# A streaming encoder step on one core: VectorE's lane marks, the sample's last v rows and the second norms

## The chip, the core and the metric

One NeuronCore of a Trainium2 chip runs the whole program in one launch. The metric is the device time of that launch in microseconds (us); below, "time" is always that. The engines are TensorE (PE; PEld is its weight load), VectorE (DVE), ScalarE (ACT), GpSimd (POOL) and SyncE (SP).

## What is computed

The reference runs one layer over a prompt of 512 frames and a sample of 64 frames with a cache of 1024 rows, width 1024, all in float32:

```python
h = x @ w_in                                   # q, k, v of 8 forgetting heads and 4 differential heads, and a gate
x = LayerNorm(alpha*x + concat(A, B) @ w_out)  # A, B: the two attentions
x = LayerNorm(alpha*x + PEER(x))               # ln2_g, ln2_b
# PEER, for each block of 128 frames
q = (xs @ w_pq).reshape(128, 8, 2, 128);  sc = einsum('thpd,hpnd->thpn', q, sub_keys)
s, i = top_k(sc, 16);  top, sel = top_k(pair sums of s, 16);  eidx = the chosen pairs' expert numbers
g = softmax(top)
hid = einsum('td,thkd->thk', xs, u_tab[eidx]);  a = g * gelu(hid)
out = einsum('thk,thkd->td', a, v_tab[eidx])   # 128 experts a frame, each a row of 1024 floats in two tables
```

Returned are y, the new k and v rows and the log forget gates.

## The kernel before

**Blocks and slots.** There are four prompt blocks (p = 0 to 3) of 128 frames and the sample (p = 4, `SMP`, 64 frames). Each prompt block needs 128 experts a frame: 128 *slots*. In the sample two experts of one frame share a pass (its 64 frames stand twice in the 128 partitions), so it has 64. That makes 576 slots. For each slot k GpSimd issues two indirect gathers of 128 rows x 4 KB = 512 KB: the u row (`peer_u`) and the v row (`peer_v`), both at line 2063. VectorE multiplies the u rows with x and sums (L1988, `hid`), ScalarE makes the coefficient (L1498, L1506) and, for slots that TensorE takes, a diagonal matrix of it (L1527). TensorE adds diag x v row into PSUM (L1173, two 128x512 matmuls, which the trace shows as four records); for the other slots VectorE adds coef x v row into `y_acc` in SBUF (L2000). Which slot goes where is `on_tensor(k)`: all 64 of the sample's go to TensorE.

**The order.** Every engine's program is one woven list. The slot lane "j" makes one step a mark: at mark j GpSimd gathers u row j and v row j-8, VectorE takes u row j-3, and row j-11 is added to the sum. All other work is cut into lanes with a fixed number of steps spread over a range of marks (`STAGES`, `SEARCH`, `spans`, `weave`): "x" the projections, "a" attention, "o"/"m" the output projection and first norm, "w" the queries and key scores, "t" VectorE's top-k search and decoding, "f" and "n" the second norm. So the lanes' marks alone set what stands between two u rows on VectorE and between two v rows on TensorE. Block p changes to p+1 at slots 128, 256, 384 and 512. "x" of block 2 makes the projections of block 2, block 3 and the sample together (`shared_tensor`): 2 steps for the gate, 16 for v, 32 for q and k, 4 empty.

**Buffers.** u rows have 6 buffers (7 from slot 288, 9 from 376), v rows 6 (9 from 282, 12 from 372). A gather waits for its buffer's last user. Weights stream on SP's queue through a ring of 5 tiles of 512 KB; the first four v tiles lie in `held`. x of the block is read by the u step from SBUF (`x1`), or, in the ranges of `MID` and from slot 408 on, from a copy in PSUM (`x_mid`, `mixer` in the trace).

**The second norm.** `f_vector` (L2015 to L2021) adds the PSUM sum to `y_acc` and takes mean and variance. PE's `n_tensor` puts gain and bias into PSUM by matmuls (L726). `n_vector` in its first step does (y - mean) x rstd over 1024 columns (L2027, L2028) and in its second waits for the gain (`ln2_row`) and does y x gain (L2031) and y + bias (L2033, L2034). SP stores y (L720). For the sample all of this stands behind the last row.

**The forgetting sums.** `sample_forget` at marks 266 to 275 takes the running sum of 1024 cached gates on VectorE (L1602).

## Time and profile before

| | |
|---|---|
| median of 3 runs | 1904.21 us (1901.42 to 1924.45) |
| profiled execution | 1909.52 us, of it 1907.7 us between first and last instruction |
| busy | PE 81%, DVE 68%, POOL 65%, ACT 32% |
| moved | 712.21 MB, mean 373 GB/s |
| mean granted clock of TensorE | 0.911 |

In the rows, busy time is in us, a bracket behind an instruction is the idle time before it and what ended it, and a stretch A:B is given in us from the first instruction. "issue" is a wait that nothing in the profile explains, "remote" one whose releaser isn't known. A gather's row is GpSimd's own time for it; its data land later.

### The profile page before, as it was taken

The numbers are of one execution on the slowest core, as the hardware profiler recorded it, in microseconds if no ns is written. First come the engines' busy times: TensorE is split into PE (matmuls) and PEld (weight loads), VectorE is DVE, ScalarE is ACT, GpSimd is POOL, SyncE is SP. The second block draws the span as 40 slices with busy tenths as digits, with TensorE's granted clock in tenths as the row PEclk, the third lists the DMA queues.
The fourth block names the chain that finished last, engine by engine and source line by source line (L and its number), as shares of the span: only waits on it lengthen the run. The fifth ranks groups of instructions, "written<-read, shape, count | busy, mean of one in ns | idle before, by whom it ended". The sixth has DMA issues, their size and how long they took to land. (4 is left out here: it accounts for less than half of the span.)

```text
span 1907.7 us, 18411 instructions
## 1 busy us (share of the span) xinstructions
PE 1542.1 (81%) x5192; PEld 819.3 (43%) x5192; DVE 1294.9 (68%) x2822; ACT 611.0 (32%) x1725; POOL 1247.6 (65%) x1199
## 2 busy tenths in 40 slices
PE   8998878959997788887979879896487776657767
PEld 7586444713454344653534534662132222222223
DVE  2378866379878775778898776778686566554443
ACT  1422363223222453234754631232232122112221
POOL 3026666677687766666677676777776666776663
PEclk9999889969998899888989989998798988888898
DMA  9899999999999999999999999999999999999995
GB/s 304 308 338 335 388 344 374 403 396 365 391 409 408 412 367 345 409 405 410 360 348 405 398 409 409 385 409 397 360 376 368 380 349 374 393 368 354 373 385 222
DMA packets 204093, 712.21 MB, mean 373 GB/s; under 512 B 24696, under 2 KB 31640, under 8 KB 203864
## 3 DMA queue, kind: packets, MB, share of 16 engines
q0 software_dynamic: 166720, 605.75, 82.5%
q1 hardware_dynamic: 37272, 105.28, 14.8%
q8 instruction: 43, 0.70, 0.1%
q14 instruction: 58, 0.48, 0.1%
HBM read 703.79 MB, written 7.74 MB: 373 GB/s over the span
## 5 line engine op out<-in xcount | busy, mean ns | idle before, releaser
L2063 POOL DMA_INDIRECT ubuf<-in_peer_u,idx x495 | 533.3, 1077 | 235.7 <-issue 146.3
L2063 POOL DMA_INDIRECT vbuf<-in_peer_v,idx x444 | 481.6, 1085 | 262.3 <-issue 115.5
L1173 PE MATMUL acc<-vbuf,diag 128*128 128x512 f32 x968 | 525.3, 677 | 140.6 <-DMA vbuf<-in_peer_v,idx 79.5
L1988 DVE CUSTOM_DVE_ANT_0 ubuf<-ubuf,x 128x1024 f32<-128x1024 f32 x304 | 369.8, 1225 | 124.3 <-DMA ubuf<-in_peer_u,idx 90.6
L1173 PEld LDWEIGHTS acc<-vbuf,diag 128*128 128x128 f32 x968 | 191.0, 212 | 387.0 <-issue 368.3
L1988 DVE CUSTOM_DVE_ANT_0 ubuf<-ubuf,mixer 128x1024 f32<-128x1024 f32 x191 | 230.1, 1217 | 109.4 <-issue 52.2
L1498 ACT ACTIVATE act_h<-hid 128x4 f32<-128x4 f32 x144 | 29.6, 205 | 537.7 <-issue 319.9
L2000 DVE SCALAR_TENSOR_TENSOR y_acc<-vbuf,coef,y_acc 128x1024 f32<-128x1024 f32 x138 | 177.3, 1285 | 34.7 <-DMA vbuf<-in_peer_v,idx 24.4
L1150 PEld LDWEIGHTS mixer<-stage,wring 128*128 128x128 f32 x1024 | 135.8, 197 | 20.5 <-issue 18.1
L1150 PE MATMUL mixer<-stage,wring 128*128 128x128 f32 (+1 forms) x1024 | 137.7, 293 | 5.7 <-issue 3.7
L1506 ACT ACTIVATE coef<-act_h,g 128x1 f32<-128x1 f32 x576 | 122.6, 283 | 17.3 <-ACT act_h L1498 1.1
L1527 ACT ACTIVATE diag<-ident,coef 128x128 f32<-128x128 f32 x320 | 115.5, 395 | 4.7 <-ACT coef L1506 0.9
L2063 POOL DMA_INDIRECT held<-in_peer_v,idx x81 | 84.1, 1038 | 36.5 <-issue 24.9
L1173 PE MATMUL acc<-held,diag 128*128 128x512 f32 x132 | 70.4, 668 | 29.7 <-DVE y_acc L2015 13.7
L1173 PE MATMUL acc<-vbuf,xT 128*128 128x512 f32 x120 | 65.1, 672 | 25.0 <-DMA vbuf<-in_peer_v,idx 13.1
L1988 DVE CUSTOM_DVE_ANT_0 wring<-wring,mixer 128x1024 f32<-128x1024 f32 x38 | 46.0, 1219 | 47.1 <-issue 16.7
L899 PE MATMUL mixer<-kv,stage 128*128 128x64 f32 (+1 forms) x320 | 49.0, 286 | 31.6 <-ACT x L1309 17.3
L778 PE MATMUL mixer<-stage,wring 128*128 128x320 f32 x256 | 71.9, 433 | 0.0
L2063 POOL DMA_INDIRECT wring<-in_peer_v,idx x51 | 48.6, 952 | 30.4 <-remote 17.0
L1498 ACT ACT_TABLE_LOAD x52 | 66.7, 1283 | 0.9
L778 PEld LDWEIGHTS mixer<-stage,wring 128*128 128x128 f32 x256 | 48.9, 191 | 26.4 <-issue 8.9
L1458 ACT COPY stage<-mixer 128x256 f32<-128x256 f32 (+1 forms) x32 | 12.8, 399 | 146.1 <-PE mixer L1150 85.7
(351 smaller groups left out, 2161.8 us busy)
## 6 DMA issues: line engine op xcount, KB each, us to landing
wring<-in_w_pq SPq DMA_DIRECT2D x64, 512.0 KB
wring<-in_w_qk SPq DMA_DIRECT2D x34, 512.0 KB
wring<-in_w_out SPq DMA_DIRECT2D x32, 512.0 KB
ubuf<-in_peer_u,idx POOLq DMA_INDIRECT x495
vbuf<-in_peer_v,idx POOLq DMA_INDIRECT x444
wring<-in_w_v SPq DMA_DIRECT2D x12, 512.0 KB
wring<-in_c_k SPq DMA_DIRECT2D x8, 512.0 KB
wring<-in_c_v SPq DMA_DIRECT2D x8, 512.0 KB
```

The lines of the kernel that those rows point to most:

```text
L778: last = pe.matmul(mixer[:, at:at + XN], w[:, c, :], xs[:, c, :], start=c == 0, stop=c == KT - 1)
L899: last = pe.matmul(head_sums(p, m, width), pT2[m % 2][:, c, :], vS[:, c, col:col + width], start=c == 0, stop=c == nk // P - 1)
L1150: last = pe.matmul(ps_o[:, t % 2, j * cols:(j + 1) * cols], w[:, c, :], x1T[:, c, :], start=c == 0, stop=c == KT - 1)
L1173: last = pe.matmul(sums[hf], diags[D_PLAN[n][0]], v_buf[b][:, hf * 512:(hf + 1) * 512], start=first, stop=last_one)
L1458: nc.scalar.copy(qh[h % 2][:, 0:2 * cols], ps_o[:, h % 2, 0:2 * cols]).then_inc(qh_out, 1)
L1498: nc.scalar.activation(act_h[:, c:c + GRP], hid[:, c:c + GRP], ACT.Gelu).then_inc(gelu_done, 1)
L1506: last = nc.scalar.activation(coef[:, c + i:c + i + 1], act_h[:, c + i:c + i + 1], ACT.Copy, scale=g[p % 2][:, at + i:at + i + 1])
L1527: nc.scalar.activation(diags[b], (ident2 if p == SMP else ident)[:, :], ACT.Copy, scale=coef[:, v % MARKS:v % MARKS + 1]).then_inc(diag_do ...
L1988: nc.vector.tensor_tensor_reduce(out=u, in0=u, in1=x, scale=1.0, scalar=0.0, op0=ALU.mult, op1=ALU.add, accum_out=hid[:, k % MARKS:k % MAR ...
L2000: nc.vector.scalar_tensor_tensor(y_acc[p % 2][:, :], v_buf[b], coef[:, v % MARKS:v % MARKS + 1], y_acc[p % 2][:, :], ALU.mult, ALU.add).th ...
L2063: pool.indirect_dma_start(buf, None, a[table], bass.IndirectOffsetOnAxis(ap=idx[p % 2][:, at:at + 1], axis=0)).then_inc(landed_, 16)
```

## The change

1. VectorE's search steps leave the marks behind a change of blocks: the third piece of block 1 runs over marks 142 to 182 (130 to 176 before), of block 2 over 270 to 308 (258 to 306), of block 3 over 399 to 440 (392 to 436), and its first two are drawn together to 350 to 366 and 366 to 384. The first norm of block 3 ("m") and the sample's stages move by 1 to 2 marks, the norm steps of block 1 are 4 marks apart instead of 1.5.
2. The 54 steps of the shared projections are spaced by weight: 18 over marks 93 to 118, 32 over 118 to 154, 4 over the rest.
3. The running sum of the cached gates is taken at marks 226 to 231 into a place of its own.
4. Of the sample's last 16 slots, the 8 odd ones go to VectorE, into block 3's `y_acc` (`y_late`). TensorE starts the sample's sum with alpha x (2 matmuls, ScalarE's pass over y falls away) and ends it with ident2 x y_late (2 matmuls).
5. The second norms are written as two passes of two halves: (y - mean) x gain, then x rstd + bias. The first now waits for `ln2_row`. The sample's reads its sum straight from PSUM, uses block 3's gain and bias, and is stored in two halves.

```diff
-SEARCH = {1: ((13, 70, 90), (21, 90, 130), (21, 130, 176)),
-          2: ((13, 211, 226), (21, 226, 258), (21, 258, 306)),
-          3: ((13, 350, 372), (21, 372, 392), (21, 392, 436))}
+SEARCH = {1: ((13, 70, 90), (21, 90, 130), (21, 142, 182)),
+          2: ((13, 211, 226), (21, 226, 258), (21, 270, 308)),
+          3: ((13, 350, 366), (21, 366, 384), (21, 399, 440))}
+SHARE = ((18, 93, 118), (32, 118, 154), (4, 154, 156.5))
+def mix_marks(lo):
+    return [lo + m for m in (2.0, 3.2, 4.4, 7.4, 8.4, 9.0)]
...
     if p == SMP:
-        return True
+        return at < DEC - 16 or at % 2 == 0
     if at < 3:
...
-          3: ((226, 231), (232, 268), (268, 275), (), (350, 436)),
-          SMP: ((266, 275), (276, 314), (314, 343), (343, 367), (436, 478))}
+          3: ((226, 231), (232, 268), (268, 277.5), (), (350, 440)),
+          SMP: ((266, 275), (278, 315), (315, 344), (344, 367), (442, 482))}
...
         out.append(("f", p, 1, end + 1.0 + late, end + 2.0 + late))
-        rows, to = ((224.0, 231.0), (368.0, 371.0), (400.0, 410.0), (end + 4.0 + late, end + 14.0 + late), (end + 4.0, end + 7.0))[p]
+        rows, to = ((224.0, 231.0), (367.5, 375.5), (400.0, 410.0), (end + 4.0 + late, end + 14.0 + late), (end + 4.0, end + 7.0))[p]
         out.append(("n", p, 2, rows, to))
...
             at = [m for piece in SEARCH[p] for m in even(*piece)]
+        elif (name, p) == ("x", SHARED):
+            at = [m for piece in SHARE for m in even(*piece)]
+        elif name == "m":
+            at = mix_marks(lo)
         elif (name, p) == ("o", SMP):
...
+        lf_sum = held[96:96 + FOX_HEADS, 0, :]
...
+        gain_s = stage[:, 0:D]
+        y_late = y_acc[(SMP - 1) % 2]
...
         def y_store(sp, p):
             frames = DEC if p == SMP else P
+            dst = o["y"][p * P:p * P + frames, :]
+            if p == SMP:
+                for hf, made in enumerate((y_half, y_done)):
+                    sp.wait_ge(made, NB if hf else 1)
+                    c = slice(hf * 512, (hf + 1) * 512)
+                    sp.dma_start(dst[:, c], y_acc[p % 2][0:frames, c]).then_inc(out_y[p % 2], 16)
+                return
             sp.wait_ge(y_done, p + 1)
-            sp.dma_start(o["y"][p * P:p * P + frames, :], y_acc[p % 2][0:frames, :]).then_inc(out_y[p % 2], 16)
+            sp.dma_start(dst, y_acc[p % 2][0:frames, :]).then_inc(out_y[p % 2], 16)
...
                         pe.wait_ge(y_done, SMP - 1)
+                        for hf in range(2):
+                            pe.matmul(sums[hf], ident_a[:, :], x1[SMP % 3][:, hf * 512:(hf + 1) * 512], start=True, stop=False)
                     elif first:
...
                         last = pe.matmul(sums[hf], diags[D_PLAN[n][0]],
-                                         v_buf[b][:, hf * 512:(hf + 1) * 512], start=first, stop=last_one)
+                                         v_buf[b][:, hf * 512:(hf + 1) * 512], start=first and p < SMP,
+                                         stop=last_one and p < SMP)
                     last.then_inc(vP_used, 1)
+                if v == JSLOTS - 1:
+                    pe.wait_ge(vD_used, JSLOTS - PE_COUNT[JSLOTS])
+                    for hf in range(2):
+                        last = pe.matmul(acc_s[hf], ident2[:, :], y_late[:, hf * 512:(hf + 1) * 512], start=False, stop=True)
+                    last.then_inc(late_done, 1)
                 yield
         def n_tensor(pe, p):
+            if p == SMP:
+                yield
+                yield
+                return
             pe.wait_ge(sc_out, HEADS * min(p + 3, SMP))
...
                             act.wait_ge(out_y[p % 2], 16 * (p // 2))
-                        nc.scalar.mul(y_acc[p % 2][:, :], x1[p % 3][:, :], ALPHA).then_inc(acc_made, 1)
+                        if p < SMP:
+                            nc.scalar.mul(y_acc[p % 2][:, :], x1[p % 3][:, :], ALPHA).then_inc(acc_made, 1)
                     if on_tensor(v):
...
         def f_scalar(act, p):
+            if p == SMP:
+                act.wait_ge(ln2_row, SMP)
+                for hf in range(2):
+                    nc.scalar.copy(gain_s[:, hf * 512:(hf + 1) * 512], ps_o[:, hf, :]).then_inc(gain_in, 1)
             act.wait_ge(ln2_v, p + 1)
...
                 if t == 2:
-                    dve.wait_ge(lf_in, 16)
                     dve.wait_ge(s_done, MATS * SMP)
-                    link(nc.vector.tensor_tensor_scan(dd[:, 0:PAST], lf_past, lf_past, 0.0, ALU.add, ALU.bypass))
-                    link(nc.vector.tensor_copy(carry[:, :], dd[:, PAST - 1:PAST]))
+                    dve.wait_ge(lf_summed, 1)
+                    link(nc.vector.tensor_copy(carry[:, :], lf_sum[:, PAST - 1:PAST]))
                     link(nc.vector.tensor_tensor_scan(dd[:, PAST:PAST + DEC], lf_wait[:, XCOLS[SMP]], lf_wait[:, XCOLS[SMP]],
...
                  yield
         def x_vector(dve, p, chain):
...
                 else:
-                    for _ in range(x_steps(p)):
-                        yield
+                    yield
+                    dve.wait_ge(lf_in, 16)
+                    nc.vector.tensor_tensor_scan(lf_sum, lf_past, lf_past, 0.0, ALU.add, ALU.bypass).then_inc(lf_summed, 1)
+                    yield
                 return
...
                     dve.wait_ge(coef_done, v // GRP + 1)
-                    if n == p * SLOTS - PE_COUNT[p * SLOTS]:
+                    first = n == p * SLOTS - PE_COUNT[p * SLOTS]
+                    if first and p == SMP:
+                        dve.wait_ge(out_y[(SMP - 1) % 2], 32)
+                    elif first:
                         dve.wait_ge(acc_made, p + 1)
...
                     dve.wait_ge(v_in[b], 16 * (nth + 1))
-                    nc.vector.scalar_tensor_tensor(y_acc[p % 2][:, :], v_buf[b], coef[:, v % MARKS:v % MARKS + 1],
-                                                   y_acc[p % 2][:, :], ALU.mult, ALU.add).then_inc(vD_used, 1)
+                    by = coef[:, v % MARKS:v % MARKS + 1]
+                    y = y_late if p == SMP else y_acc[p % 2]
+                    if first and p == SMP:
+                        nc.vector.tensor_scalar(y[:, :], v_buf[b], by, None, ALU.mult).then_inc(vD_used, 1)
+                    else:
+                        nc.vector.scalar_tensor_tensor(y[:, :], v_buf[b], by, y[:, :], ALU.mult, ALU.add).then_inc(vD_used, 1)
                 yield
         def f_vector(dve, p, chain):
...
             end = min((p + 1) * SLOTS, JSLOTS)
-            dve.wait_ge(vP_used, PE_COUNT[end])
-            wait(dve, vD_used, end - PE_COUNT[end])
             if p == SMP:
-                dve.wait_ge(acc_made, NB)
-            if p == SMP:
-                for hf in range(2):
-                    last = nc.vector.tensor_tensor(y[:, hf * 512:(hf + 1) * 512], y[:, hf * 512:(hf + 1) * 512], acc_s[hf], ALU.add)
+                dve.wait_ge(late_done, 1)
+                sums = acc_s
             else:
-                last = nc.vector.tensor_tensor(y[:, :], y[:, :], acc[:, :], ALU.add)
-            last.then_inc(acc_read, 1)
-            dve.wait_ge(acc_read, p + 1)
+                dve.wait_ge(vP_used, PE_COUNT[end])
+                wait(dve, vD_used, end - PE_COUNT[end])
+                nc.vector.tensor_tensor(y[:, :], y[:, :], acc[:, :], ALU.add).then_inc(acc_read, 1)
+                dve.wait_ge(acc_read, p + 1)
+                sums = [y[:, hf * 512:(hf + 1) * 512] for hf in range(2)]
             for hf in range(2):
-                last = nc.vector.bn_stats(stats2[:, n, hf, :], y[:, hf * 512:(hf + 1) * 512])
+                last = nc.vector.bn_stats(stats2[:, n, hf, :], sums[hf])
             link(last)
...
         def n_vector(dve, p, chain):
             link, y, n = chain.link, y_acc[p % 2], p % 2
+            gain, bias_n = (ps_o2, acc_p) if p >= SMP - 1 else (ps_s[:, 0:D], acc_s)
+            dve.wait_ge(ln2_v, p + 1)
+            if p == SMP:
+                dve.wait_ge(out_y[p % 2], 16 * (p // 2))
+                dve.wait_ge(gain_in, 2)
+            else:
+                dve.wait_ge(ln2_row, p + 1)
+            for hf in range(2):
+                c = slice(hf * 512, (hf + 1) * 512)
+                was, by = (acc_s[hf], gain_s[:, c]) if p == SMP else (y[:, c], gain[:, c])
+                link(nc.vector.scalar_tensor_tensor(y[:, c], was, mv2[:, n, 0:1], by, ALU.subtract, ALU.mult))
             dve.wait_ge(ln2_r, p + 1)
             link(nc.vector.reciprocal(rstd2[:, n, 1:2], rstd2[:, n, 0:1]))
-            link(nc.vector.tensor_scalar(y[:, :], y[:, :], mv2[:, n, 0:1], rstd2[:, n, 1:2], ALU.subtract, ALU.mult))
-            yield
-            dve.wait_ge(ln2_row, p + 1)
-            link(nc.vector.tensor_tensor(y[:, :], y[:, :], ps_o2 if p >= SMP - 1 else ps_s[:, 0:D], ALU.mult))
-            bs = acc_p if p >= SMP - 1 else acc_s
-            link(nc.vector.tensor_tensor(y[:, 0:512], y[:, 0:512], bs[0], ALU.add))
-            nc.vector.tensor_tensor(y[:, 512:D], y[:, 512:D], bs[1], ALU.add).then_inc(y_done, 1)
+            yield
+            for hf in range(2):
+                c = slice(hf * 512, (hf + 1) * 512)
+                last = nc.vector.scalar_tensor_tensor(y[:, c], y[:, c], rstd2[:, n, 1:2], bias_n[hf], ALU.mult, ALU.add)
...
+            last.then_inc(y_done, 1)
             yield
...
```

The first place is VectorE about the end of block 1 (its PSUM sum is read at L2015, L2063 after); `y_acc1` is block 1's sum, `sc`, `top_v`, `best_i`, `cand` are the search. Before:

```order
L2000 SCALAR_TENSOR_TENSOR y_acc0<-vbuf,coef,y_acc0 128x1024 [waits v_in4,acc_made,coef_done]
L1893 MAX top_v<-sc 128x8 [waits sc_out] x2
L1885 MAX_INDEX best_i<-best_v,cand2 128x8
L1897 TENSOR_TENSOR cand<-top_v 128x256
L2015 TENSOR_TENSOR y_acc1<-y_acc1,acc 128x1024 [waits vD_used,vP_used,dve_link]
L2019 BN_STATS stats2<-y_acc1 128x6 [waits acc_read]
L2019 BN_STATS stats2<-y_acc1 128x6
L2021 BN_AGGR mv2<-stats2 128x2 [waits dve_link]
L1988 ISA ubuf,hid<-ubuf,x1_2 128x1024 [waits u_in1]
L1988 ISA hid 128x1
L2000 SCALAR_TENSOR_TENSOR y_acc0<-vbuf,coef,y_acc0 128x1024 [waits v_in5,vD_used,coef_done]
```

After:

```order
L2051 SCALAR_TENSOR_TENSOR y_acc0<-vbuf,coef,y_acc0 128x1024 [waits v_in4,acc_made,coef_done]
L2063 TENSOR_TENSOR y_acc1<-y_acc1,acc 128x1024 [waits vD_used,vP_used]
L2067 BN_STATS stats2<-y_acc1 128x6 [waits acc_read]
L2067 BN_STATS stats2<-y_acc1 128x6
L2069 BN_AGGR mv2<-stats2 128x2 [waits dve_link]
L2031 ISA ubuf,hid<-ubuf,x1_2 128x1024 [waits u_in1]
L2031 ISA hid 128x1
L2051 SCALAR_TENSOR_TENSOR y_acc0<-vbuf,coef,y_acc0 128x1024 [waits v_in5,vD_used,coef_done]
L2031 ISA ubuf,hid<-ubuf,x1_2 128x1024 [waits u_in2]
L2031 ISA hid 128x1
L2051 SCALAR_TENSOR_TENSOR y_acc0<-vbuf,coef,y_acc0 128x1024 [waits v_in0,vD_used,coef_done]
L1643 COPY carry<-held 8x1 [waits lf_summed,s_done]
```

The search rows ahead of the sum are gone, and the scan has become a copy (L1643); the slots' own rows stand as they did, and the search is taken up again three u rows later.

The second place is VectorE at mark 225, the first step of block 0's norm, with what each instruction waits for. Before:

```order
L1988 ISA ubuf,hid<-ubuf,x1_1 128x1024 [waits u_in0,pick_done]
L1988 ISA hid 128x1
L2027 RECIPROCAL rstd2<-rstd2 128x1 [waits ln2_r]
L2028 TENSOR_SCALAR y_acc0<-y_acc0,mv2,rstd2 128x1024 [waits dve_link]
L1988 ISA ubuf,hid<-ubuf,x1_1 128x1024 [waits u_in1,dve_link]
L1988 ISA hid 128x1
L2000 SCALAR_TENSOR_TENSOR y_acc1<-vbuf,coef,y_acc1 128x1024 [waits v_in5,vD_used,coef_done]
L1893 MAX top_v<-sc 128x8 [waits sc_out] x2
```

After:

```order
L2031 ISA ubuf,hid<-ubuf,x1_1 128x1024 [waits u_in0,pick_done]
L2031 ISA hid 128x1
L2084 SCALAR_TENSOR_TENSOR y_acc0<-y_acc0,mv2,mixer 128x512 [waits ln2_row,ln2_v]
L2084 SCALAR_TENSOR_TENSOR y_acc0<-y_acc0,mv2,mixer 128x512 [waits dve_link]
L2086 RECIPROCAL rstd2<-rstd2 128x1 [waits ln2_r,dve_link]
L2031 ISA ubuf,hid<-ubuf,x1_1 128x1024 [waits u_in1,dve_link]
L2031 ISA hid 128x1
L2051 SCALAR_TENSOR_TENSOR y_acc1<-vbuf,coef,y_acc1 128x1024 [waits v_in5,vD_used,coef_done]
L1936 MAX top_v<-sc 128x8 [waits sc_out] x2
```

Before, `ln2_row` was awaited four u rows later, at L2031; now it is awaited ahead of them. The scan of the cached gates (L1663) has come in behind the second step.

The third place is VectorE's end: the last u rows and the sample's norm. Before:

```order
L1988 ISA wring,hid<-wring,mixer 128x1024 [waits x_copied,u_in8]
L1988 ISA hid 128x1
L2013 TENSOR_TENSOR y_acc0<-y_acc0,mixer 128x512 [waits acc_made,vD_used,vP_used]
L2013 TENSOR_TENSOR y_acc0<-y_acc0,mixer 128x512
L2019 BN_STATS stats2<-y_acc0 128x6 [waits acc_read]
L2019 BN_STATS stats2<-y_acc0 128x6
L2021 BN_AGGR mv2<-stats2 128x2 [waits dve_link]
L2027 RECIPROCAL rstd2<-rstd2 128x1 [waits ln2_r]
L2028 TENSOR_SCALAR y_acc0<-y_acc0,mv2,rstd2 128x1024 [waits dve_link]
L2031 TENSOR_TENSOR y_acc0<-y_acc0,mixer 128x1024 [waits ln2_row,dve_link]
L2033 TENSOR_TENSOR y_acc0<-y_acc0,acc 128x512 [waits dve_link]
L2034 TENSOR_TENSOR y_acc0<-y_acc0,acc 128x512 [waits dve_link]
```

After:

```order
L2051 SCALAR_TENSOR_TENSOR y_acc1<-held,coef,y_acc1 128x1024 [waits v_in6,vD_used,coef_done]
L2051 SCALAR_TENSOR_TENSOR y_acc1<-held,coef,y_acc1 128x1024 [waits v_in8,vD_used,coef_done]
L2051 SCALAR_TENSOR_TENSOR y_acc1<-vbuf,coef,y_acc1 128x1024 [waits v_in1,vD_used,coef_done]
L2051 SCALAR_TENSOR_TENSOR y_acc1<-vbuf,coef,y_acc1 128x1024 [waits v_in3,vD_used,coef_done]
L2051 SCALAR_TENSOR_TENSOR y_acc1<-vbuf,coef,y_acc1 128x1024 [waits v_in5,vD_used,coef_done]
L2067 BN_STATS stats2<-mixer 128x6 [waits late_done]
L2067 BN_STATS stats2<-mixer 128x6
L2069 BN_AGGR mv2<-stats2 128x2 [waits dve_link]
L2084 SCALAR_TENSOR_TENSOR y_acc0<-mixer,mv2,stage 128x512 [waits gain_in,out_y0,ln2_v]
L2084 SCALAR_TENSOR_TENSOR y_acc0<-mixer,mv2,stage 128x512 [waits dve_link]
L2086 RECIPROCAL rstd2<-rstd2 128x1 [waits ln2_r,dve_link]
L2090 SCALAR_TENSOR_TENSOR y_acc0<-y_acc0,rstd2,acc 128x512 [waits dve_link]
```

Five v rows stand behind the last u row, the sum is awaited once (`late_done`), and the passes over y between the sum and the store have become four of half the width.

## Rows read from the trace of the kernel before

**Rows 1.** The page, part 2: GB/s in 40 slices of the span

```profile
GB/s 304 308 338 335 388 344 374 403 396 365 391 409 408 412 367 345 409 405 410 360 348 405 398 409 409 385 409 397 360 376 368 380 349 374 393 368 354 373 385 222
```

**Rows 2.** Stretches: length, busy PE, PEld, DVE, ACT, POOL (instructions), clock, DMA share, GB/s

```profile
440.00:480.00 40.00, 40.00 (x86) 13.54 (x87) 36.88 (x90) 13.06 (x35) 31.34 (x26) 1.00 0.95 347
...
960.00:1010.00 50.00, 37.15 (x96) 17.46 (x95) 46.56 (x107) 25.60 (x54) 38.92 (x34) 0.86 0.97 353
1310.00:1340.00 30.00, 23.52 (x48) 8.28 (x47) 23.35 (x81) 5.95 (x19) 23.29 (x23) 0.98 1.00 385
1340.00:1370.00 30.00, 12.53 (x24) 4.75 (x22) 18.83 (x46) 7.55 (x19) 20.50 (x21) 0.82 0.95 358
1370.00:1410.00 40.00, 31.94 (x64) 12.94 (x64) 39.52 (x101) 14.87 (x50) 31.44 (x28) 0.84 0.95 351
...
1840.00:1860.00 20.00, 12.48 (x26) 4.44 (x26) 9.40 (x17) 4.37 (x17) 14.05 (x15) 1.00 1.03 412
```

**Rows 3.** GpSimd's gathers by buffer, 1800 to 1860: busy us, mean ns, idle

```profile
L2063 POOL DMA_INDIRECT ubuf<-in_peer_u,idx x15 | 14.1, 937 | 4.6 <-issue 4.0 <-DVE hid L1988 0.6
```

**Rows 4.** Timeline of GpSimd at 1360: start, us, idle before

```profile
1361.70 0.94 POOL L2063 DMA_INDIRECT ubuf<-in_peer_u,idx  x1 [1.98 <-DVE hid L1988]
...
1364.78 0.94 POOL L2063 DMA_INDIRECT ubuf<-in_peer_u,idx  x1 [0.90 <-DVE hid L1988]
```

**Rows 5.** Timeline: VectorE's first norm step, TensorE's gain and bias, blocks 0 to 3; the scan

```profile
845.06 0.16 DVE L2027 RECIPROCAL rstd<-rstd 128x1 f32<-128x1 f32 x1
...
847.51 4.16 PE L726 MATMUL mixer<-d_neg,ident 32*128 32x512 f32 x8
...
1285.04 0.15 DVE L2027 RECIPROCAL rstd<-rstd 128x1 f32<-128x1 f32 x1
...
1284.06 3.81 PE L726 MATMUL mixer<-d_neg,ident 32*128 32x512 f32 x8
...
1390.02 0.15 DVE L2027 RECIPROCAL rstd<-rstd 128x1 f32<-128x1 f32 x1
...
1388.34 3.69 PE L726 MATMUL mixer<-d_neg,ident 32*128 32x512 f32 x8
...
1752.30 0.16 DVE L2027 RECIPROCAL rstd<-rstd 128x1 f32<-128x1 f32 x1
...
1756.23 1.87 PE L726 MATMUL acc<-d_neg,ident 32*128 32x512 f32 x4
...
981.10 2.28 DVE L1602 TENSOR_TENSOR_SCAN d_neg<-held 8x1024 f32<-8x1024 f32 x1
```

**Rows 6.** Timeline of the end: a late gather, TensorE's last rows, VectorE's norm, the store

```profile
1873.51 0.93 POOL L2063 DMA_INDIRECT held<-in_peer_v,idx  x1 [0.31 <-issue]
...
1881.57 5.39 PE L1173 MATMUL mixer<-held,xT 128*128 128x512 f32 x12 [2.12 <-DMA held<-in_peer_v,idx]
...
1886.80 10.46 PE L1173 MATMUL mixer<-vbuf,diag 128*128 128x512 f32 x24
...
1897.30 1.28 DVE L2013 TENSOR_TENSOR y_acc<-y_acc,mixer 128x512 f32<-128x512 f32 x2 [15.72 <-PE mixer L1173]
1898.62 1.29 DVE L2019 BATCH_NORM_STATS2 stats<-y_acc 128x6 f32<-128x512 f32 x2
...
1900.51 0.16 DVE L2027 RECIPROCAL rstd<-rstd 128x1 f32<-128x1 f32 x1 [0.36 <-ACT rstd L1533]
...
1903.53 0.69 DVE L2034 TENSOR_TENSOR y_acc<-y_acc,acc 128x512 f32<-128x512 f32 x1
1904.25 0.49 SPq L720 DMA_DIRECT2D out_y<-y_acc  x1
```

**Rows 7.** Timeline of VectorE: a v row, and a wait whose releaser isn't known

```profile
1372.24 1.28 DVE L2000 SCALAR_TENSOR_TENSOR y_acc<-wring,coef,y_acc 128x1024 f32<-128x1024 f32 x1
...
1783.63 1.22 DVE L2031 TENSOR_TENSOR y_acc<-y_acc,mixer 128x1024 f32<-128x1024 f32 x1 [18.46 <-remote]
```

**Rows 8.** Timeline of TensorE: one v row after a long wait

```profile
1374.71 3.78 PE L1173 MATMUL acc<-held,diag 128*128 128x512 f32 x4 [13.70 <-DVE y_acc L2015]
```

17 lines of the change are left out of this document (12 added, 5 removed).

## The prediction

> **What bounds the kernel now.** I read the page first, for its 40 slices. In nearly half of them the DMA engines move over 385 GB/s, and no slice goes above 412 [rows 1]. The best stretches do the same: 412 between 1840 and 1860 us [rows 2]. I take 410 as full speed. The slots read 1152 gathers of 512 KB, so one gather is 524288 B / 410 GB/s = 1.28 us of transfer and a slot 2.56. All 712.21 MB would take 1737 us; the profiled execution takes 1909.52. So the kernel is bound by its transfers, and what can be won is the 170 us in which they fall short of 410. A stretch loses its length x (1 - GB/s / 410). That is the scale for everything below: taking an instruction off VectorE, TensorE or ScalarE wins nothing by itself, only what it gives back to the gathers.
>
> Next I read the stretches with low GB/s, with each engine's busy time [rows 2]. 440 to 480 us (slots 98 to 111) loses 6.1 us, 960 to 1010 (slots 264 to 280) loses 50 x (1 - 353/410) = 7.0, 1310 to 1340 loses 1.8, 1340 to 1370 loses 3.8 and 1370 to 1410 loses 5.8 (together slots 378 to 412). The engine to watch is GpSimd. A gather costs it 0.937 us and 0.31 us of "issue" before the next [rows 3]: 4.6 us idle for 15, or 1.24 us each, just under the 1.28 of the transfer. But in the losing stretches a gather takes longer: 31.34/26 = 1.205 us, 38.92/34 = 1.145, 31.44/28 = 1.123, 23.29/23 = 1.013 [rows 2]. With 0.31 added, the first makes 1.52 us, and 26 x 1.52 = 39.4 of 40 us: GpSimd is full. What differs is VectorE: there it takes x from SBUF beside the u row, in 1840 to 1860 from PSUM, and it is busy 36.88 of 40 us instead of 9.40 of 20.
>
> The Trainium skill (page "SBUF — State Buffer", section "Who interferes with whom") says that VectorE and GpSimd share one pair of ports under an exclusive lock, which VectorE takes when it reads two operands from SBUF. The 1.205 against 0.937 us agree with it. By that rule only VectorE's instructions with two SBUF operands would matter, not its busy share. I keep to the measured means.
>
> Two other views close this part. GpSimd's own timeline shows where VectorE's u rows come late: waits of 1.98 and 0.90 us at 1360 [rows 4]. And from 1440 on every 30 to 40 us some engine stands still without a releaser; the longest row is VectorE's 18.46 us before the second norm step of block 3, though TensorE's gain was written at 1758.10 [rows 5, 7].
>
> **The change, part by part.**
>
> (A) Shared projections. Between 440 and 480 TensorE is busy 40.00 of 40 us, and GpSimd is full too [rows 2]. 18 steps over marks 93 to 118 instead of 21 marks take load off TensorE per slot, at most the 6.1 us lost there. But GpSimd stays full as long as VectorE holds it up, and the part gets 4 slots longer, each 3.03 us instead of 2.56, or with what is denser behind it about +1.5. I take 0 (from -6.1 to +1.5): with two engines full, relief of one gives nothing.
>
> (B) Change from block 1 to block 2. The search rows leave VectorE for marks 270 to 308, and the scan of 2.28 us [rows 5] goes. Nothing is less in sum; the work comes where u rows leave room. If a gather there fell from 1.145 to 1.013 us, the least loaded of these stretches, that is 34 x 0.132 = 4.5 us. The ends are 0 and -7.0, all that is lost. Not all of it is VectorE's, as TensorE's rows are awaited too (37.15 of 50 us busy, at clock 0.86): -3.5.
>
> (C) Change from block 2 to block 3. VectorE's backlog at 1340 to 1370 (2.9 us of waits, [rows 4]) came with the second search piece over 372 to 392 and the third from 392 on. Now the second ends at 384 and nothing follows until 399. The waits go (-2.9). 28 gathers from 1.123 to 1.013 would be -3.1, but from slot 399 on the third piece is as dense as before, so I take half, -1.6. Against that marks 366 to 384 are denser, which I charge with 1.5, about half of what the piece's waits cost before. Sum -3. The ends are -11.4 (the three stretches together) and +2.
>
> (D) The norms' first step now waits for the gain. It began at 845.06, 1285.04, 1390.02 and 1752.30 us, and TensorE's gain and bias ended at 847.51 + 4.16 = 851.67, 1287.87, 1392.03 and 1758.10 [rows 5]. So the new waits would be 6.6, 2.8, 2.0 and 5.8 us, 17.2 in sum. Behind the waiting instruction VectorE's u row is queued; that frees the buffer the next gather waits for. The cover is the u buffers: 6 x 2.56 = 15.4 us, of which a gather's landing takes up 8.06 (issued 1873.51, used 1881.57, [rows 6]), leaves 7.3, more with 7 or 9 buffers. All four waits are below it, the first by 0.7 only. While VectorE waits, GpSimd is undisturbed; afterwards VectorE has to catch up. The passes get shorter: from the reciprocal to the last pass 1900.51 to 1904.22 is 3.71 us, four half passes of 0.69 and 0.16 are 2.92, so 0.8 less a norm [rows 6]. The scan's 2.28 us now stand at marks 226 to 231, behind the longest of the waits. I take +1.5, from -1 to +17.2 (each wait paid in full).
>
> (E) The end. TensorE takes the last nine rows from 1881.57 to 1897.26, 1.74 us each [rows 6], slower than they arrive: the last should land at 1881.57 + 8 x 1.28 = 1891.8. With every second row on VectorE at 1.28 us [rows 7] both keep up: last row done at 1893.1, two closing matmuls of a row's price, 1894.8, where VectorE's sum began at 1897.30: -2.4. From there before: 6.92 us to 1904.22. Now: statistics and aggregate 1.53 (1898.62 to 1900.51 less the 0.36 wait), four half passes 2.76, reciprocal 0.16, 0.1 of gaps: 4.55, so -2.4. Together -4.8, rounded -5. The first half of the store can leave 0.7 us sooner, which is worth nothing if the second half ends last. Ends: -5.5; and 0, if the closing matmuls run at the low clock, where a row took 3.78 us instead of 1.74 [rows 8] (+2.0), and GpSimd's last 12 gathers cost 1.205 instead of 0.937 us (+3.2), because VectorE again reads two SBUF operands beside them. The cover of the latter is the 8 us that a gather waits in the queues.
>
> Sum: 0 - 3.5 - 3 + 1.5 - 5 = -10. The profiled execution would take 1899.5. It stands 5.3 above the median of the runs, 1904.21, so on the median 1894.
>
> **The rivals.**
>
> (R1) Only the tail is gained. The stretches at the changes of blocks lose because GpSimd is near full all along, and VectorE's work, moved by ten slots, holds up other gathers instead. For it: the change of blocks at slots 128 to 142 (about 530 to 575 us) had a search piece over it too, and its slice, the twelfth, has 409 GB/s [rows 1]; work is moved, not removed. Against: 2.9 us of waits stand right behind a backlog. Time: 1904.2 - 5 = 1899. It also covers that the unexplained standstills move by some microseconds either way.
>
> The Trainium skill (page "Runtime: NRT & Kernel Launch", section "Instruction fetch mechanics") says that crossing a block of the instruction stream is "mostly hidden". By that rule the standstills are something else and would not move with the count of instructions; the 18.46 us without a releaser [rows 7] at least shows no other cause. It would not alter the sum.
>
> (R2) Slower: VectorE parks before the gain. One mechanism: `ln2_row` is awaited ahead of u rows on an in-order engine. If the u buffers are mostly empty of slack when it waits (GpSimd near full, VectorE behind), each wait passes on in full. It decides once the wait exceeds the slack, 7.3 us at best and less where VectorE is late already. Price: 17.2 - 3 x 0.8 for the shorter passes - 5 for the tail, nothing gained at the changes: +9.8, 1914.
>
> (R3) All of it is gained: 6.1 + 7.0 + 11.4 + 5.5 = 30, 1874. For it: if VectorE's density is what makes gathers long, each stretch has the same cause. Against: at 440 to 480 and 960 to 1010 TensorE is the other full or slow engine.
>
> **How the numbers follow.** The forecast has 0.53 (own range 1884 to 1902, from (B) to (D) each half way to an end), R1 0.22, R2 0.11, R3 0.14. The range takes in R1 whole, and R2 and R3 in part: 1877 to 1906. A measurement of this kernel can tell about 2% from no change, 38 us. Even R3 stays inside with 30 us. Faster by over 2%: 0.03, for R3 with the standstills going too; slower 0.02, for R2 with a backlog that never clears; within 2%: 0.95.
>
> **What would show it.** (B) right: at slots 264 to 280 a gather near 1.01 us and over 380 GB/s. (C) right: no waits of GpSimd for VectorE near slot 390, over 370 GB/s over slots 378 to 412. (D) right: VectorE waits 2 to 7 us at L2084 and GpSimd shows no wait for it in the next 10 us; wrong if such waits and fewer than 380 GB/s follow. (A) right: slots 93 to 118 still near 347 GB/s. (E) right: the chain ends with TensorE's closing matmuls about 3 us after the last landing, then 4.6 us of VectorE. The prediction is wrong as a whole if the time is above 1904, or if the profile loses over 10 us in a stretch that ran full before, slots 112 to 125 or 366 to 384 above all.

## The result: 0.6% slower, not 0.5% faster

| | before | changed |
|---|---|---|
| median of 21 runs each, taken together | 1912.37 us (1900.98 to 1932.49) | 1924.88 us (1910.16 to 1938.54) |
| ratio, with 95% interval | | 1.0061 (1.0037 to 1.0085) |
| profiled execution's span | 1907.7 us | 1915.5 us |
| last gather issued, to the end | 23.9 us | 18.4 us |

Two later comparisons of the same two kernels gave 1.0043 and 1.0053. I had forecast 10 us less; it is 8 to 12 us more. The median of before is 1912 over 21 runs; the 1904 of the forecast was that of three.

The page's slices of the changed kernel answer to [rows 1]:

```profile
PE 1536.1 (80%) x5160; PEld 809.4 (42%) x5160; DVE 1301.2 (68%) x2829; ACT 603.9 (32%) x1714; POOL 1250.4 (65%) x1199
...
GB/s 302 294 349 339 396 349 372 410 395 371 410 409 409 412 370 385 409 402 378 344 357 379 391 381 409 357 409 366 335 392 361 366 365 367 358 411 354 347 385 276
```

Busy times are those of before within 1.3%. No engine has more to do; the time went into stretches with fewer GB/s. To find them I set the start times of GpSimd's gathers side by side, slot by slot: at slot 152 the changed kernel is 12 us ahead of before, at slot 256 5 ahead, at 320 2 behind, at 400 13 behind, and so it stays to the last gather (+13). The end gives 5.5 back. A single profile is noisy by some microseconds in such a stretch, so below I use the means over the profiles of all kernels that share a part, with their range.

The stretches, as in [rows 2] (length, busy PE, PEld, DVE, ACT, POOL, clock, DMA share, GB/s):

```profile
436.00:476.00 40.00, 40.00 (x87) 13.54 (x86) 35.68 (x86) 12.08 (x33) 32.07 (x27) 1.00 1.00 367
...
954.00:1002.00 48.00, 33.73 (x91) 14.33 (x89) 38.47 (x83) 22.70 (x54) 36.31 (x33) 0.96 0.97 361
...
1340.00:1370.00 30.00, 22.49 (x44) 8.96 (x44) 23.47 (x40) 11.89 (x36) 24.53 (x18) 0.85 0.89 296
1370.00:1420.00 50.00, 36.63 (x69) 13.99 (x70) 34.07 (x79) 13.06 (x42) 39.00 (x37) 0.86 1.01 392
```

954 to 1002 is slots 264 to 280, the place of term (B): a gather costs 36.31/33 = 1.100 us, not the 1.01 I hoped for. 1340 to 1370 is the place of term (C) and got worse: 24.53/18 = 1.363 us a gather and 296 GB/s; before it was 358. The stretch behind it got better, 392 GB/s where before had 351.

Where VectorE waits for TensorE's gain (timeline; in brackets the idle time before and its releaser):

```profile
840.58 1.53 DVE L2084 SCALAR_TENSOR_TENSOR y_acc<-y_acc,mv,mixer 128x512 f32<-128x512 f32 x2 [4.63 <-PE mixer L750]
...
1303.00 1.53 DVE L2084 SCALAR_TENSOR_TENSOR y_acc<-y_acc,mv,mixer 128x512 f32<-128x512 f32 x2 [10.33 <-issue]
```

GpSimd behind the second of them, and TensorE ahead of it:

```profile
1307.12 1.74 POOL L2122 DMA_INDIRECT ubuf<-in_peer_u,idx  x1 [4.95 <-DVE hid L2031]
```

```profile
1292.03 3.75 PE L1199 MATMUL acc<-vbuf,diag 128*128 128x512 f32 x4 [2.09 <-DMA vbuf<-in_peer_v,idx]
1295.71 7.19 PE L750 MATMUL mixer<-d_neg,ident 32*128 32x512 f32 x8
```

I had priced the second wait at 2.8 us; it is 10.33. TensorE reached its gain group late, behind a v row that it had to await, and the group ran at the low clock, 7.19 us instead of the 3.81 of [rows 5]. The stretch of the group, as in [rows 2]:

```profile
1295.70:1302.90 7.20, 7.20 (x10) 2.56 (x9) 0.00 (x0) 0.00 (x0) 4.94 (x6) 0.50 1.03 409
```

The granted clock is 0.50, the lower of its two levels, after two waits of TensorE for v rows. The transfers run at 409 GB/s, as fast as in the best stretches: GpSimd goes on while VectorE stands, and from 1254 to 1302 us nothing but its own issue holds it. So the v row that TensorE awaited was still in transfer, and not late through VectorE. Then GpSimd has no free u buffer and waits 4.95 us. That is the mechanism of rival R2, VectorE parked before the gain and the wait passed on.

A backlog of VectorE, grouped by line, 1349 to 1362 us (slots 388 to 391), VectorE and then GpSimd:

```profile
L2031 DVE CUSTOM_DVE_ANT_0 ubuf<-ubuf,x 128x1024 f32<-128x1024 f32 x7 | 8.2, 1218 | 0.0
L2031 DVE CUSTOM_DVE_ANT_0 wring<-wring,x 128x1024 f32<-128x1024 f32 x2 | 2.4, 1217 | 0.0
L2031 DVE CUSTOM_DVE_ANT_0 held<-held,x 128x1024 f32<-128x1024 f32 x1 | 1.2, 1224 | 0.0
```

```profile
L2122 POOL DMA_INDIRECT vbuf<-in_peer_v,idx x4 | 6.4, 1609 | 1.2 <-issue 0.6 <-PE acc L1199 0.6
L2122 POOL DMA_INDIRECT ubuf<-in_peer_u,idx x2 | 3.7, 1846 | 0.6 <-issue 0.6
L2122 POOL DMA_INDIRECT held<-in_peer_u,idx x1 | 2.0, 1990 | 0.3 <-issue 0.3
```

VectorE takes ten u rows nearly back to back, and a gather costs GpSimd 1.61 to 1.99 us on average by buffer instead of 0.94. This backlog comes with block 3's search marks and not with the wait for the gain. At slots 388 to 393 a gather takes 1.51 us on average here and 1.49 to 1.53 in the runs e2, e5 and g2 below, which have these marks and await the gain late; in e1, e3, f2 and f3, which await it early and have the search where it was, it takes 0.96 to 1.35. Nor is it lasting: with these marks slots 384 to 400 take 50.7 us (49.7 to 52.6, 7 profiles) against 45.9 (42.6 to 48.8, 9 profiles), and slots 400 to 416 give it back, 43.5 against 48.3.

### The profile page after: what moved, and what is told of

The parts are those of the page before. It is cut to its first block and busy times, and to the rows that moved or that the text cites. A ratio compares the mean times of both kernels' runs of the same rounds, so it can differ in the third digit from the quotient of the medians.

```text
span 1915.5 us, 18344 instructions
## 1 busy us (share of the span) xinstructions
PE 1536.1 (80%) x5160; PEld 809.4 (42%) x5160; DVE 1301.2 (68%) x2829; ACT 603.9 (32%) x1714; POOL 1250.4 (65%) x1199
## 5 line engine op out<-in xcount | busy, mean ns | idle before, releaser
L2122 POOL DMA_INDIRECT ubuf<-in_peer_u,idx x495 | 540.2, 1091 | 256.0 <-issue 140.4
L2122 POOL DMA_INDIRECT vbuf<-in_peer_v,idx x444 | 475.4, 1071 | 263.7 <-issue 117.7
L1199 PE MATMUL acc<-vbuf,diag 128*128 128x512 f32 x968 | 518.9, 669 | 141.4 <-DMA vbuf<-in_peer_v,idx 99.7
L2031 DVE CUSTOM_DVE_ANT_0 ubuf<-ubuf,x 128x1024 f32<-128x1024 f32 x305 | 371.3, 1225 | 134.7 <-DMA ubuf<-in_peer_u,idx 99.1
L2031 DVE CUSTOM_DVE_ANT_0 ubuf<-ubuf,mixer 128x1024 f32<-128x1024 f32 x190 | 229.6, 1217 | 120.4 <-DMA ubuf<-in_peer_u,idx 50.9
L2051 DVE SCALAR_TENSOR_TENSOR y_acc<-vbuf,coef,y_acc 128x1024 f32<-128x1024 f32 x142 | 182.5, 1285 | 26.8 <-DMA vbuf<-in_peer_v,idx 20.8
L1542 ACT ACTIVATE coef<-act_h,g 128x1 f32<-128x1 f32 x576 | 122.8, 283 | 16.5 <-issue 0.4
L2031 DVE CUSTOM_DVE_ANT_0 wring<-wring,mixer 128x1024 f32<-128x1024 f32 x38 | 46.1, 1219 | 31.0 <-issue 14.0
L896 PE MATMUL mixer<-kv,q_pad 128*128 128x128 f32 (+3 forms) x128 | 48.4, 461 | 11.4 <-DVE neg_max L1726 9.5
```

The lines of the kernel that those rows point to most:

```text
L896: last = pe.matmul(dst, q_pad[:, g_, half, :], kT[:, g_, 0:nk], start=True, stop=not fox)
L1199: last = pe.matmul(sums[hf], diags[D_PLAN[n][0]], v_buf[b][:, hf * 512:(hf + 1) * 512], start=first and p < SMP, stop=last_one and p < SMP)
L1542: last = nc.scalar.activation(coef[:, c + i:c + i + 1], act_h[:, c + i:c + i + 1], ACT.Copy, scale=g[p % 2][:, at + i:at + i + 1])
L2031: nc.vector.tensor_tensor_reduce(out=u, in0=u, in1=x, scale=1.0, scalar=0.0, op0=ALU.mult, op1=ALU.add, accum_out=hid[:, k % MARKS:k % MAR ...
L2051: nc.vector.scalar_tensor_tensor(y[:, :], v_buf[b], by, y[:, :], ALU.mult, ALU.add).then_inc(vD_used, 1)
L2122: pool.indirect_dma_start(buf, None, a[table], bass.IndirectOffsetOnAxis(ap=idx[p % 2][:, at:at + 1], axis=0)).then_inc(landed_, 16)
```

## The experiments

All were timed beside before on their own chip; a ratio is to be read against that. The first eight and the last six ran on chips on which before takes 1912 to 1915 us, e9 to e12 on one on which it takes 1837. Line numbers differ by kernel.

**e1, the code parts with before's tables.** The changed kernel, `SEARCH`, `STAGES`, `MID` and the norm marks as before, `SHARE` and `mix_marks` gone.

> The changed kernel with all tables of marks as before (search pieces, stages, shared projections, first norm of block 3, norm steps of block 1): the new second norms, the wait for the gain in their first step, the moved running sum and the sample's last v rows on VectorE stay. Theory T (the tables cost the time, above all the search piece drawn together to marks 366 to 384): no cost is left but the tail's gain, so 4 to 6 us faster than before. Theory N (VectorE parked before the gain, my rival R2): 5 to 15 us slower than before.

1.0045 (1.0014 to 1.0076). The code parts are slower by themselves although they hold the tail's gain. Repeated as f3:

> The changed kernel with all tables of marks as before. With the dips 5 to 12 us slower than before, again. Without them theory N1 expects 3 to 6 us faster (the tail), theory N2 5 us slower.

1.0015 (0.9982 to 1.0047). Together some 0.3%, less than e1 alone said.

**e2, the tables with before's code.**

> The kernel before with the changed tables of marks alone. Theory T: all of the loss is here and the tail's gain is missing, so 12 to 20 us slower than before. Theory N: within 4 us of before.

1.0011 (0.9978 to 1.0045): no 12 us. In it lie a gain and a loss, as the next runs and the table below show.

**e3 and e4, the changed kernel with one block's marks back.** e3 takes the norm marks of block 1 back too, e4 those of block 3's first norm and of the sample's stages.

```diff
-          3: ((13, 350, 366), (21, 366, 384), (21, 399, 440))}
+          3: ((13, 350, 372), (21, 372, 392), (21, 392, 436))}
```

> The changed kernel with block 3's search pieces and block 1's norm steps back at their marks (350, 372, 392, 436 and 368 to 371). Theory T: the dense search piece is the cause, so GpSimd's gathers of 1.9 us and more near slot 390 go and the time falls by 6 to 14 us against the changed kernel, to before or a little below. Theory N: no change, still 8 to 14 us above before.

```diff
-          2: ((13, 211, 226), (21, 226, 258), (21, 270, 308)),
+          2: ((13, 211, 226), (21, 226, 258), (21, 258, 306)),
```

> The changed kernel with the third search piece of block 2 back at marks 258 to 306, and the first norm of block 3 and the sample's stages back at theirs. Theory T: slots 280 to 312, where the changed kernel's profile falls 8 us behind, come back by 4 to 8 us. Theory N: no change. A third theory, that such differences are the unexplained standstills falling otherwise in each kernel, expects no change here and in the run before.

1.0022 (0.9992 to 1.0052) and 1.0023 (0.9991 to 1.0055). Each is some 0.3% below the changed kernel's 1.0043 to 1.0061, no more than the width of one interval, so by the times alone only likely. In e4's profile slots 304 to 320 take 50.3 us, in e3's 61.5.

**e5 and g2, the changed kernel with the prompt blocks' norms as before** (first step: y - mean times rstd; second step: await the gain, then gain and bias; five passes). g1 is the changed kernel beside g2 on one chip.

> The changed kernel with the prompt blocks' second norm written as before (first step without the gain, the gain awaited in the second step, five passes). Theory N (the wait for the gain in the first step sets VectorE back and GpSimd then waits for its u rows): 7 to 13 us faster than the changed kernel, so at before or up to 3 us below, and no wait of VectorE for TensorE's gain of over 1 us. Theory C (the moved running sum, or the tail, costs the time): within 4 us of the changed kernel, 8 to 15 us above before.

> The changed kernel again. On a chip with the dips (before near 1912 us) 5 to 12 us slower than before. On one without (before near 1837) the parts as measured there (wait 0.5, block 2's marks 0, block 3's marks 1, tail and shared projections together -12 us) add to 8 to 12 us faster than before.

> The changed kernel with the prompt blocks' norms as before. Theory N within the changed kernel: with the dips 5 to 11 us faster than the run beside it; without them within 2 us of it. Rival (the earlier gap of 0.5% was noise between chips): within 3 us of it with the dips too.

e5: 1.0009 (0.9977 to 1.0041). g1: 1.0053 (1.0018 to 1.0087). g2: 0.9964 (0.9926 to 1.0002). On one chip the new norms cost 0.9% of the changed kernel by the two ratios, while the medians of g1 and g2 lie 11.4 us (0.6%) apart. From both pairs (1.0061 and 1.0009, 1.0053 and 0.9964) it is 0.7% on average, 13 us. This is the largest part. g1's profile shows one such wait whole (VectorE, TensorE, GpSimd):

```profile
849.37 1.53 DVE L2084 SCALAR_TENSOR_TENSOR y_acc<-y_acc,mv,mixer 128x512 f32<-128x512 f32 x2 [9.91 <-PE mixer L750]
```

```profile
838.39 3.75 PE L1199 MATMUL acc<-vbuf,diag 128*128 128x512 f32 x4 [2.33 <-DMA vbuf<-in_peer_v,idx]
842.08 7.19 PE L750 MATMUL mixer<-d_neg,ident 32*128 32x512 f32 x8
849.20 8.15 PE L1199 MATMUL acc<-vbuf,diag 128*128 128x512 f32 x12
```

```profile
844.30 0.93 POOL L2122 DMA_INDIRECT vbuf<-in_peer_v,idx  x1 [0.30 <-issue]
852.64 1.74 POOL L2122 DMA_INDIRECT ubuf<-in_peer_u,idx  x1 [7.41 <-DVE hid L2031]
```

VectorE stands 9.91 us; GpSimd runs out of buffers and issues nothing for 7.41.

**e6, e7, e8: the two parts that gain.** e6 is before with the sample's part (late v rows, norm, store), e7 before with `SHARE` and block 1's third piece over 142 to 182, e8 both.

> The kernel before with the sample's part alone: every second of its last 16 v rows on VectorE, its sum begun and ended by TensorE, its norm in two passes of halves, its store in halves. My term (E): 4 to 6 us faster than before, all of it after the last gather. Rival: VectorE's late v rows hold GpSimd's gathers up, and nothing is left of it (within 2 us).

> The kernel before with the shared projections spaced by weight and the third search piece of block 1 over marks 142 to 182, nothing else. By the profiles so far slots 112 to 144 come 7 us earlier: 4 to 8 us faster than before, if the lead is kept. My term (A) of 0 expects within 2 us of before. A third view, that a lead is given back later because GpSimd and the queues wait elsewhere: the lead is there at slot 144 and gone at slot 250.

> Both of the last two together on the kernel before. If the gains add: 8 to 14 us faster than before. If leads are given back: no more than the tail's 4 to 6 us.

0.9996 (0.9961 to 1.0032), 0.9982 (0.9948 to 1.0016), 0.9944 (0.9907 to 0.9980). Only e8 is clear of 1; the single ones are inconclusive by the times. The profiles tell them apart: slots 112 to 144 take 95.4 us on average with `SHARE` (93.8 to 97.4, 11 profiles) and 101.2 without (99.0 to 103.1, 5 profiles), no overlap. From the last gather to the end is 17.6 us on average with the new tail (16.5 to 18.4, 12 profiles), 20.5 with the old one (23.9, 20.0, 19.2, 18.9).

**e9 and f2, the wait alone.** Before, with one wait at the head of `n_vector`:

```diff
+            if p < SMP:
+                dve.wait_ge(ln2_row, p + 1)
             dve.wait_ge(ln2_r, p + 1)
```

> The kernel before with one wait more: VectorE awaits TensorE's gain and bias in the first step of the four prompt blocks' norms. Theory N: 7 to 13 us slower than before, most of it in slots 224 to 256 and 336 to 384, with GpSimd waiting for VectorE's u rows behind the wait. Rival (the two-pass form of half passes and the moved running sum cost the time): within 3 us of before.

> The kernel before with the early wait for the gain alone. On a chip with the dips theory N expects 7 to 13 us slower than before, its rival (running sum and two passes) within 3 us. On a chip without them within 2 us, as before.

1.0003 (0.9989 to 1.0018) on the chip of 1837 us, 1.0007 (0.9979 to 1.0036) on one of 1915. Both miss what I expected of theory N: the wait alone costs no 7 us in the end. VectorE does wait; in e9's profile:

```profile
825.13 0.16 DVE L2029 RECIPROCAL rstd<-rstd 128x1 f32<-128x1 f32 x1 [6.44 <-PE mixer L726]
```

**e10 and e11, one block's marks alone on before,** on that faster chip.

> The kernel before with the third search piece of block 2 over marks 270 to 308 and the marks of the first norm of block 3 and of the sample's stages as changed. Theory T2 (the piece's decoding, passes of 1.22 us, now stands right behind VectorE's wait for the sample's last scores): slots 304 to 320 take 9 to 12 us longer, some of it gained before and after, 3 to 8 us slower than before. My term (B): 0 to 7 us faster.

> The kernel before with block 3's search pieces over marks 350 to 366, 366 to 384 and 399 to 440. By the profiles so far slots 384 to 400 take 6 us longer and 400 to 416 take 6 us less: within 3 us of before. My term (C): 3 us faster, at most 11. A rival by which the dense piece alone costs: 4 to 8 us slower.

1.0000 (0.9986 to 1.0013) and 1.0007 (0.9995 to 1.0020). There neither costs anything that can be told; the 3 to 8 us that I had expected of theory T2 for e10 did not come. What differs between the chips is plain in stretches from 1500 to 1600 us, of before and then of e9 on the faster chip:

```profile
1500.00:1600.00 100.00, 72.61 (x142) 27.55 (x141) 64.25 (x156) 23.86 (x84) 67.19 (x71) 0.90 0.96 367
```

```profile
1500.00:1600.00 100.00, 72.09 (x142) 25.07 (x141) 63.31 (x111) 22.38 (x79) 75.89 (x80) 0.97 1.03 409
```

The two programs differ only in the early wait; one moves 367 GB/s here, the other 409. The dips every 30 to 40 us are not in the kernel; what makes them no row shows.

**e12 and f4, the best version:** `SHARE` and the new tail, and the prompt blocks' norms in the two-pass form, but all in the second step.

```diff
         def n_vector(dve, p, chain):
+            if p < SMP:
+                yield
...
-            yield
+            if p == SMP:
+                yield
```

> Tail and shared projections as in the changed kernel, all else as before, but the prompt blocks' norms in two passes of halves with all of them in the second step, so that the gain is awaited as late as before. If shorter passes help where VectorE is full: 1 to 4 us faster than the kernel with tail and shared projections alone, 8 to 15 us faster than before. If passes beside the gathers cost nothing: the same as that kernel, 6 to 12 us faster than before. If one wait with four passes in a row behind it sets VectorE back: slower than that kernel by 2 us or more.

> Tail, shared projections and two-pass norms with the gain awaited late: 8 to 15 us faster than before on either kind of chip, 0.990 to 0.996 of it.

0.9934 (0.9920 to 0.9949) and 0.9958 (0.9930 to 0.9985): 12 and 8 us faster than before on the two kinds of chip. The two passes are harmless once the gain is awaited late. Whether they gain anything over e8 stays open; the two were not run on one chip.

f1, the changed kernel once more:

> The changed kernel itself. If this chip is one with the recurring dips (before near 1912 us): 8 to 15 us slower than before, as measured. If it is one without (before near 1837): theory N1, that the loss needs the dips (VectorE's wait eats the slack that a dip then needs), expects within 3 us of before, or faster by the tail's and the shared projections' 10 us; theory N2, that the loss is of the order of instructions alone, expects 8 us slower there too.

1.0043 (1.0011 to 1.0075), on a chip of 1915 us. The changed kernel was never run on the faster kind, so that it would gain there is only argued.

## Why the prediction was wrong, point by point

The gathers' means by slots, over the 16 profiles from chips with the dips, are these. The stretches were picked after looking at the profiles:

| part | slots | with | without | difference |
|---|---|---|---|---|
| shared projections (A) | 112 to 144 | 95.4 (93.8 to 97.4) | 101.2 (99.0 to 103.1) | -5.8 |
| gain awaited early, block 0 (D) | 224 to 256 | 105.5 (101.1 to 108.9) | 97.6 (95.5 to 99.8) | +7.9 |
| block 2's marks, with those of block 3's first norm and the sample's stages (B) | 280 to 366 | 280.2 (274.4 to 290.3) | 273.4 (268.1 to 279.2) | +6.8 |
| early gain with block 3's marks (C, D) | 366 to 416 | 152.0 (149.5 to 153.9) | 147.0 (143.2 to 153.8), the 12 others | +5.0 |
| tail (E) | to the end | 17.6 (16.5 to 18.4) | 20.5 (18.9 to 23.9) | -2.9 |

The sum is +11.0 us; the three ratios of the changed kernel make +8 to +12. Added up for each of the other twelve runs on these chips, the parts lie within the interval of eleven; f2, the wait alone, is the exception.

**(A), taken at 0, is -5.8.** I argued that with two engines full the relief of one gives nothing. It does give, nearly the whole of the end that I had named, -6.1. In 436 to 476 us TensorE is still busy 40.00 of 40, at 367 GB/s where before had 347. Most of the gain stands just behind: slots 112 to 118 take 17.9 us (17.1 to 18.8) with `SHARE` and 22.3 (22.0 to 22.7) without. There, in before, GpSimd waits three times until TensorE gives back a v buffer, and TensorE has up to 12 matmuls of the projections between two v rows:

```profile
484.48 1.09 POOL L2063 DMA_INDIRECT vbuf<-in_peer_v,idx  x1 [2.12 <-PE acc L1173]
...
492.03 0.99 POOL L2063 DMA_INDIRECT vbuf<-in_peer_v,idx  x1 [2.74 <-PE acc L1173]
...
499.58 0.96 POOL L2063 DMA_INDIRECT vbuf<-in_peer_v,idx  x1 [2.24 <-PE acc L1173]
```

```profile
484.05 5.80 PE L767 MATMUL mixer<-wring,stage 128*128 128x512 f32 x12
489.77 1.98 PE L1173 MATMUL acc<-vbuf,diag 128*128 128x512 f32 x4
491.60 5.80 PE L767 MATMUL mixer<-wring,stage 128*128 128x512 f32 x12
```

The changed kernel has every second of these groups half as long there (2.88 us for 6), and one wait of 2.1 us instead of three. `SHARE` and block 1's third search piece were not tried apart, but these 4.4 us lie ahead of mark 130, where that piece began before, so they are `SHARE`'s. How the rest divides stays open.

**(B), taken at -3.5, is +6.8.** The step was "the work comes where u rows leave room". At slots 280 to 304 it does (74.1 us on average with these marks, 76.9 without); but the decoding of the experts, the last steps of the piece, now falls on marks 299 to 308, around a wait of VectorE for the sample's scores and bias. The changed kernel's profile:

```profile
1081.02 1.29 DVE L1769 CUSTOM_DVE_ANT_0 kv<-mixer,bias 128x1088 f32<-128x1088 f32 x1 [7.21 <-remote]
...
1084.58 1.22 DVE L1971 TENSOR_TENSOR sc<-pick,iota 128x1024 f32<-128x1024 uint32 x1
1085.84 1.22 DVE L1975 TENSOR_TENSOR sc<-sc,top_i 128x1024 f32<-128x1024 f32 x1
```

```profile
1083.74 1.74 POOL L2122 DMA_INDIRECT ubuf<-in_peer_u,idx  x1 [5.40 <-DVE hid L2031]
```

VectorE comes out of a wait of 7.21 us and has passes of 1.22 us before it instead of u rows. Slots 304 to 320 take 57.7 us on average with these marks (49.3 to 61.5, 7 profiles), 49.7 without (47.8 to 54.9, 9 profiles). The length goes with the wait, and not with the decoding alone: in six of the seven VectorE waits 4.50 to 7.21 us there, and the slots take 55.1 to 61.5; in g1 and in e10, on the faster chip, no such wait is over 2.3 us, and they take 49.3 and 50.2 with the same decoding. Before has the wait as well (7.03 us, at 1056.03), but ahead of slot 304; slots 280 to 320 together are 131.8 us with these marks and 126.6 without. What the wait is for the row does not name. TensorE's last scores ended at 1075.89, so it is likely the bias, which SyncE's queue had been given at 1066.9.

**(C), taken at -3, is nothing or a loss.** Block 3's marks alone give 146.2 us for slots 366 to 416, the kernels with neither part 147.8, too close to tell. With the early gain beside them it is 152.0, in all four profiles more than in any of the seven with one part alone, though two of the five with neither have 151.0 and 153.8. Where the wait itself stands, at slots 366 to 384, the four are apart from all others: 57.4 us (56.4 to 58.2) against 53.0 (50.8 to 55.6). VectorE waits 8.35 to 10.33 us there in these four and 1.86 to 6.29 in the four with the early gain alone. Block 1's first norm step stands only one u row later than before; new around it are the search piece drawn together to marks 366 to 384 and the norm steps further apart. e3 took both back at once, so which of them lengthens the wait is not shown. I had charged each alone and never the two together.

**(D), taken at +1.5, is the step that failed:** it cost +7.9 in block 0 and, together with (C), +5.0 in block 1. Its waits were priced from TensorE's end in before's profile, each against VectorE's start: 6.6 and 2.8 us for the first two. The three profiles of the changed kernel show 4.63, 6.66 and 9.91 for block 0, 8.35 to 10.33 for block 1 and 5.67 to 6.02 for block 2, which I had at 2.0. (Block 3's are 19.67 to 23.01, but before has 18.46 in its second step too [rows 7].) Block 0's 6.6 was right as long as TensorE's gain group ran at the high clock (4.06 us in f1, and a wait of 6.66); at the low one it took 7.19 (g1, and a wait of 9.91). In block 1 TensorE began its group 3.0 to 4.8 us after VectorE had come to a stand, where in before it began 1.0 us ahead of VectorE's step. And the cover was set at 7.3 us, six buffers of 2.56 less 8.06 for the landing. But VectorE does not take a row when it lands: at slots 223 to 230 of before it took it 8.3 to 12.4 us after the gather was issued, as the order has it three marks behind. 15.4 less 10.3 on average and 1.2 for the row itself leaves 4 us, and with the 12.4 of slot 223, the row parked first, 2. The waits themselves say the same: GpSimd's is shorter than VectorE's by 2.5 us in g1, f1, f3 and e4, and by 3.2 to 4.5 in e1, e3, e9 and f2. That VectorE lags is what the marks say, and I had read them. Block 0's waits in the eight profiles with the early gain are 4.63 to 9.92 us, 7.9 on average, and slots 224 to 256 take 7.9 longer: in place they are paid about in full. The running sum, which now stands there too, has little part in it, as e5 and g2 keep it and take 97.8 and 99.8 us.

R2 had the mechanism, and a chance of 0.11; its price of 17.2 for four waits came out at 7.9 and a share of 5.0 for two, and nothing that can be told for the last two, where there are nine buffers (slots 416 to the last take 452.9 us, 451.7 in the others). That its +9.8 is near the measured +8 to +12 is partly luck: it charged the waits too high, took -2.4 for shorter passes, which no run shows, and -5 for the tail, and left out (A) and (B), which nearly cancel.

Against this stands that the wait alone (e9, f2) costs nothing in the times. In f2's profile slots 224 to 256 take 104.9 us, as in the others with the early gain, so the local loss is there; the interval of f2 leaves up to 0.36%, 7 us. The 13 us between the changed kernel and its twin with the old norms thus hold the wait, its meeting with block 3's marks, and perhaps more. How they divide I can't say from these runs.

**(E), taken at -5, is -2.9,** on the faster chip -4.4 (34.2 to 29.7). The mechanism is right; the profile of before that I started from had an unusually long tail (23.9, where the three others with the old tail have 18.9 to 20.0), and against those three the gain is 1.8. The end now reads:

```profile
1904.51 1.28 DVE L2051 SCALAR_TENSOR_TENSOR y_acc<-vbuf,coef,y_acc 128x1024 f32<-128x1024 f32 x1 [1.20 <-DMA vbuf<-in_peer_v,idx]
1905.85 1.98 PE L1206 MATMUL mixer<-y_acc,ident 128*128 128x512 f32 x4 [0.60 <-DVE y_acc L2051]
1907.87 1.29 DVE L2067 BATCH_NORM_STATS2 stats<-mixer 128x6 f32<-128x512 f32 x2 [2.08 <-PE mixer L1206]
...
1911.21 1.41 DVE L2090 SCALAR_TENSOR_TENSOR y_acc<-y_acc,rstd,acc 128x512 f32<-128x512 f32 x2
1911.99 1.15 SPq L741 DMA_DIRECT2D out_y<-y_acc  x2
```

VectorE's last row starts as its data land, the closing matmuls take 1.98 us (1.73 foreseen), and from the statistics to the end of the last pass are 4.75 us (4.55 foreseen). VectorE's late rows hardly held the gathers up: the last twelve v gathers take 1.00 us on average with the new tail and 0.94 with the old one, 0.8 us in all.

As for ports, the Trainium skill (page "SBUF — State Buffer", section "Who interferes with whom") says that a VectorE instruction with two inputs in SBUF contends with a GpSimd instruction that reads SBUF. The ten u rows above, with two SBUF operands each, beside gathers of 1.61 to 1.99 us, agree with it if the gather reads its `idx` in SBUF meanwhile. I had weighed the rule and then kept to mean times. As shown above, this backlog is not what made the kernel slower.
